# A two-layer gated mixer and expert kernel: half of the first parameters as a TensorE row, their slots loaded earlier, norms moved into the attention sweeps and from GpSimd to VectorE

## What is computed

```python
c_act = jax.nn.silu(c)
for l in range(DEPTH):
    mod = c_act @ ada_w[l] + ada_b[l]
    sh1, sc1, gt1, sh2, sc2, gt2 = jnp.split(mod, 6, axis=-1)
    h = modulate(rmsnorm(x, norm_mix[l]), sh1, sc1)
    proj = h @ w_in[l]
    y_a = hgrn2_mixer(...)   # gated linear recurrence
    y_b = mla_mixer(...)     # latent attention, rmsnorm of q and k per head, then rope
    y_c = diff_mixer(...)    # differential attention, rmsnorm of q, k and of the output
    y_d = swa_mixer(...)     # sliding window, rmsnorm of q and k
    merged = jnp.sum(sigmoid(gates) * branch, axis=2)
    x = x + gt1 * (merged @ w_out[l])
    h2 = modulate(rmsnorm(x, norm_ffn[l]), sh2, sc2)
    x = x + gt2 * moe(h2, ...)
```

## Time and profile before

| | us |
|---|---|
| median of 3 runs (2461.95 to 2464.5) | 2462.12 |
| the profiled execution | 2463.01 |
| its span (first to last instruction) | 2461.3 |
| PE busy | 2312.6 |
| DVE busy | 1416.3 |
| ACT busy | 1004.6 |
| POOL busy | 495.6 |

### The profile page before, as it was taken

The page is one execution under the profiler, slowest core; times in us unless marked ns, Lnnn a source line. Parts: engine busy times, 40 slices in busy tenths (PEclk is TensorE's granted clock), DMA queues, the critical chain, the costliest instruction groups (busy, mean ns, idle before and its releaser), DMA issues.

```text
span 2461.3 us, 33198 instructions
## 1 busy us (share of the span) xinstructions
PE 2312.6 (94%) x12222; PEld 1761.7 (72%) x12222; DVE 1416.3 (58%) x2621; ACT 1004.6 (41%) x1865; POOL 495.6 (20%) x457
## 2 busy tenths in 40 slices
PE   5999999988899999999989999999798999999997
PEld 4897787886575466777668978778766744677775
DVE  6637765554644634666486376654555455356664
ACT  2523333534443123666424233344444422246662
POOL 1002235011000210444200023330200022014440
PEclk9999999999999999999999999999898999999999
DMA  8322232231216653766272222321221284526652
GB/s 254 101 80 73 81 100 80 71 108 56 73 56 219 214 195 123 278 236 239 100 250 88 82 77 87 121 73 59 75 78 56 77 287 161 222 94 252 242 193 109
DMA packets 202110, 333.73 MB, mean 136 GB/s; under 512 B 31200, under 2 KB 162144, under 8 KB 185696
## 3 DMA queue, kind: packets, MB, share of 16 engines
q1 hardware_dynamic: 179024, 305.32, 36.5%
q0 software_dynamic: 19296, 19.98, 2.6%
q10 hardware_dynamic: 3632, 6.31, 0.7%
HBM read 352.48 MB, written 51.38 MB: 164 GB/s over the span
## 4 chain that ended last, share of the span: by engine, by line
PE 82%; DVE 7%; ACT 3%; issue 2%; SPq 2%; DMA 2%; POOL 1%; POOLq 0%; DVEq 0%; ACTq 0%
PE ps L733 77%; PE ps L731 6%; DVE ring_rounded L1799 1%; SPq L569 1%; DVE ssq L1911 1%; DMA ring<-in_ada_w 1%; DVE nmax L1936 1%; SPq L592 1%; DVE spare L1781 0%; DVE H L1894 0%; DVE H_rounded L1904 0%; DVE ps L1933 0%; DMA ring<-in_w_in 0%; ACT WH_rounded L1364 0%; DVE SQKV L1913 0%
## 5 line engine op out<-in xcount | busy, mean ns | idle before, releaser
L733 PE MATMUL ps<-H_rounded,WH_rounded 128*128 128x512 f32 x768 | 308.4, 402 | 0.0
L733 PE MATMUL ps<-X_rounded,WH_rounded 128*128 128x512 f32 x640 | 287.2, 449 | 9.9 <-DVE ring_rounded L1799 3.6
L1799 DVE TENSOR_TENSOR ring_rounded<-ring,WH_rounded 128x512 fp32r<-128x512 f32 (+2 forms) x168 | 198.2, 1188 | 152.9 <-ACT WH_rounded L1364 152.1
L733 PE MATMUL ps<-WH_rounded,X_rounded 128*128 128x256 f32 (+1 forms) x960 | 273.0, 284 | 6.9 <-issue 6.9
L733 PE MATMUL ps<-ring_rounded,X_rounded 128*128 128x256 f32 (+1 forms) x960 | 271.2, 282 | 0.0
L733 PE MATMUL ps<-WH_rounded,H_rounded 128*128 128x256 f32 (+1 forms) x960 | 271.1, 282 | 0.0
L733 PE MATMUL ps<-X_rounded,ring_rounded 128*128 128x512 f32 x640 | 253.5, 396 | 0.0
L1364 ACT ACTIVATE WH_rounded<-ring 128x512 fp32r<-128x512 f32 (+2 forms) x168 | 163.6, 983 | 184.9 <-PE ps L733 66.9
L733 PE MATMUL ps<-Y,ring 128*128 128x512 f32 x512 | 221.2, 593 | 1.9 <-ACT Y L1462 1.9
L733 PE MATMUL ps<-lmask,ident 128*128 128x256 f32 x784 | 190.8, 400 | 5.1 <-issue 3.1
L733 PEld LDWEIGHTS ps<-WH_rounded,X_rounded 128*128 128x128 f32 x960 | 184.1, 192 | 9.7 <-issue 9.6
(11 more groups left out here) (365 smaller groups left out, 4552.6 us busy)
## 6 DMA issues: line engine op xcount, KB each, us to landing
ring<-in_w_in SPq DMA_DIRECT2D x272, 256.0 KB, 3.9
ring<-in_ada_w SPq DMA_DIRECT2D x128, 256.0 KB, 4.9
Y<-in_moe_w_down SPq DMA_DIRECT2D x18, 1024.0 KB
ring<-in_w_branch SPq DMA_DIRECT2D x64, 256.0 KB, 5.2
ring<-in_moe_w_down SPq DMA_DIRECT2D x14, 1024.0 KB, 7.1
gate_logits<-CM SPq DMA_DIRECT2D x44, 256.0 KB, 2.6
...
```

Source lines behind the costliest of these rows:

```text
L733: ins = nc.tensor.matmul(o, lhsT, rhs, start=start, stop=stop)
L1799: ins = v.tensor_tensor(low[j][:, at:at + size], ring[:, j, at:at + size], high[i][:, at:at + size].bitcast(F32), ALU.subtract)
```

## The change

**Start of a layer.** The columns of shift stay with DVE (`ada` with two pairs instead of four); the columns of scale are made by PE as a row: `mod_part` multiplies one column of `cact` by 256 columns of a slot, eight matmuls a slot, four slots; ACT copies the row out of banks 7 and 6; `row_section` turns it into columns. The columns of the eight slots are dealt anew (`ADA_COLUMNS`). For layer 1, slots 0 to 3 are loaded by SP at the end of layer 0's expert stage, ahead of the rows that it loads back, and DVE's first pair and PE's first part are done there.

**Norms.** All gain multiplications and rope go to DVE (`weigh_by`, `rope`, with tables of `rope_tables`); for q and k pairs the two gains are multiplied once and applied to k alone. The norms `dif_norm`, `swa_norm` and `dif_post` leave `SCHEDULE` and are done inside the sweeps (`NORM_IN_SWEEP`), as is the pair `("ada", 3)` (`ADA_IN_SWEEP`, one k step every second unit).

**Banks and order.** `mla_turn` uses banks 2 to 5 in place of 2 and 3, without dummy matmuls between; product `c` 5 moves ahead of `turn` 2; `swa_turn` moves behind the sweep DIFF; `ada_keys(3, 2)` comes ahead of `d` in the ring.

```diff
 SCHEDULE = [("hg_norm", 0), ("c", 0), ("ada", 0), ("c", 1), ("hg_y", 0), ("c_norm", 0), ("ada", 1), ("c", 2),
             ("c_turn", 0), ("up", 0), ("c", 3), ("up", 1), ("turn", 0), ("c", 4),
-            ("up", 2), ("turn", 1), ("up", 3), ("turn", 2), ("section", 2), ("ada", 2), ("c", 5), ("turn", 3),
-            ("sweep", MLA), ("dif_norm", 0), ("d", 0), ("dif_norm", 1), ("ada", 3), ("d", 1), ("dif_norm", 2),
-            ("d", 2), ("dif_norm", 3), ("mla_y", 0), ("swa_norm", 0), ("swa_norm", 1),
-            ("swa_norm", 2), ("section", 3), ("swa_norm", 3), ("dif_turn", 0), ("swa_turn", 0),
-            ("sweep", DIFF), ("dif_post", 0), ("sweep", SWA), ("dif_y", 0), ("swa_y", 0)]
-WARM = {("c", 2): 4, ("up", 0): 7, ("turn", 2): 5, ("d", 2): 22}
+            ("up", 2), ("turn", 1), ("up", 3), ("c", 5), ("turn", 2), ("section", 2), ("ada", 2), ("turn", 3),
+            ("sweep", MLA), ("d", 0), ("d", 1), ("mla_y", 0), ("d", 2), ("section", 3), ("dif_turn", 0),
+            ("sweep", DIFF), ("swa_turn", 0), ("sweep", SWA), ("dif_y", 0), ("swa_y", 0)]
+WARM = {("c", 2): 5, ("up", 0): 7, ("turn", 2): 2, ("turn", 3): 3, ("c", 1): 3}
...
...
               + [("c", 4), ("c", 5)] + ada_keys(3, 0) + gate_keys("mla")
-              + [("d", 0), ("d", 1)] + ada_keys(3, 2) + [("d", 2)] + gate_keys("diff") + gate_keys("swa")
+              + ada_keys(3, 2) + [("d", 0), ("d", 1), ("d", 2)] + gate_keys("diff") + gate_keys("swa")
...
+ADA_COLUMNS = (0, 1, 4, 5, 2, 3, 6, 7, *range(8, 24))
+NORM_IN_SWEEP = {"mla": {23: ("dif_norm", 0), 25: ("dif_norm", 1), 27: ("dif_norm", 2), 29: ("dif_norm", 3)},
+                 "diff": {1: ("swa_norm", 0), 2: ("swa_norm", 1), 3: ("swa_norm", 2), 6: ("swa_norm", 3),
+                          9: ("dif_post", 0), 12: ("dif_post", 1), 15: ("dif_post", 2)},
+                 "swa": {3: ("dif_post", 3)}}
+ADA_IN_SWEEP = {8 + 2 * k: k for k in range(8)}
...
@@ sync: behind the expert weights, ahead of y_two @@
+                if l + 1 < DEPTH:
+                    for i in range(RING):
+                        ring_at = {j: at for at, j in slot_ring.items()}[ring_place(l + 1, ("ada", i))[0]]
+                        b, m = max(at for at in RELEASES if (3 * at[0] + at[1]) % SLOTS == ring_at)
+                        eng.wait_ge(expert_used, p.so_far(expert_used) - len(RELEASES) + RELEASES.index((b, m)) + 1)
+                        alone()
+                        ada_load(l + 1, ("ada", i))
...
@@ tensor @@
+            def mod_part(l, n):
+                half, i = divmod(n, 2)
+                b = 7 - half
+                w, used = slot(row_keys(half)[i], l)
+                w = heads(w, NC)
+                if i == 0:
+                    free(b)
+                for k in range(NC):
+                    ins = mm(ps[0:1, b, i * 256:(i + 1) * 256], cact[:, k:k + 1], w[:, k], k == 0, k == NC - 1,
+                             last=i == 1 and k == NC - 1)
...
+            def row_section(b):
+                free(b)
...
+                for m in range(NC):
+                    ins = mm(ps[:, b, m:m + 1], mod_row[:, tt(m)], ones[0:1, 0:1], last=last)
...
                 if l == 0:
                     warm(4, 5)
+                    for n in range(2):
+                        mod_part(0, n)
                 for c in range(NC):
                     square_sum(c)
-                for s in range(2):
-                    warm(((7, 37), (22, 30))[l][s], 5)
-                    section(1, s)
+                for n in range(2 if l == 0 else 1, 4):
+                    mod_part(l, n)
+                warm(3, 5)
+                section(1, 1)
+                row_section(1)
...
+                if l + 1 < DEPTH:
+                    mod_part(l + 1, 0)
                 for t in range(NT):
-                    warm((20, 2, 2, 2)[t], 7)
+                    warm((13 if l + 1 < DEPTH else 20, 2, 2, 2)[t], 2)
...
@@ tensor, mla_turn @@
                 for f in range(4):
-                    b = 2 + f % 2
-                    if f == 2 and t in (0, 1):
-                        warm((5, 8)[t], 5)
+                    b = 2 + f
...
@@ vector, in sweep @@
+                    if s.kind == "mla" and n in ADA_IN_SWEEP:
+                        ada(3, 2, ks=[ADA_IN_SWEEP[n]])
...
+                    if n - 1 in NORM_IN_SWEEP[s.kind]:
+                        norm_in_sweep(*NORM_IN_SWEEP[s.kind][n - 1])
...
+            def norm_in_sweep(step_, t):
+                head_norm(*norm_of(step_, t))
+                if step_ == "dif_norm":
+                    weigh_by(heads(DQK[:, t, 512:1024], 8), repeat(row("diff_qk_norm", 0, HD), 8), gained)
+                elif step_ == "swa_norm":
+                    weigh_by(heads(SQKV[:, t, 512:640], 2), repeat(row("swa_qk_norm", 0, HD), 2), gained)
+                else:
+                    weigh_by(heads(y_tok["diff"][:, t], DH), repeat(row("diff_onorm"), DH), gained)
...
@@ vector, do: hg_norm, c_norm, up @@
+                        head_norm(*norm_of(step_, t))
+                        weigh_by(heads(hgO[:, t], HEADS), repeat(row("hg_onorm"), HEADS), vector_step)
+                        eng.wait_ge(vector_step, p.given(vector_step))
+                        weigh_by(hgO[:, t], TM[:, t, 512:1024], gained)
...
+                    head_norm(*norm_of(step_, 1))
+                    weigh_by(CM[:, :, QR:QR + KVR], repeat(row("mla_kv_norm"), NT), gained)
+                    rope_tables()
...
+                    weigh_by(qk[:, HEADS:, 0:NOPE], repeat(row("mla_qk_norm", 0, NOPE), HEADS), vector_step)
+                    rope(qk, i)
```

200 lines of the change are left out of this document (105 added, 95 removed).

## The result

| | before | after |
|---|---|---|
| median, us | 2464.5 (2458.56 to 2469.11, 7 runs) | 2451.57 (2444.28 to 2452.13, 7 runs) |
| ratio, 95% interval | | 0.9942 (0.9929 to 0.9955) |
| PE busy in the span, us | 2312.6 of 2461.3 | 2293.7 of 2450.4 |
| POOL busy, us | 495.6 | 341.5 |
| share of PE in the chain that ended last | 82% | 79% |

Faster, as forecast, but by 0.6% where 1.7% was forecast: 2451.57 us lies above the range of 2397 to 2446. To find out where the rest went I read the starts and ends of the stages from the timelines of PE in both traces (first and last matmul of each), for both layers. The forecast stands beside each.

A forecast was written before the change was run, and what follows sets the result against it. PE was taken as the bound (82% of the last chain). Per layer -23.9 - 9.5 + 5.0 + 4.5 + 3.3 + 5.1 = -15.5, twice -31.0, with layer 1's start -40.5: 2421.5 us, range 2397 to 2446.

The forecast's parts named there:

- From MLA to DIFF, minus 23.9: MLA's last values to DIFF's first scores: without norms, PE's work runs together, 74.0 us become 50.1, per layer.
- Moving one pair of ada slots up in the ring is free by the same reason: Weight ring: d 1's slot, though freed only when the sweep ends, is ready within d 0's 11.8 us; cost nothing.
- SWA, minus 9.5: First four SWA units: 19.1 us become 9.1, with 0.5 kept for dif_post 3, per layer.
- Norms in MLA, plus 5.0: Late MLA units: four norms make PE wait about 1.3 us in each of three, 1.1 at the end; bounds 0, 14.8.
- Norms in DIFF, plus 4.5: DIFF sweep: four swa_norms at 0.6 us and three dif_posts at 0.7, per layer; between 0 and 18.
- rival "slower": Norms in sweeps cost full length because ACT holds the next exponentials back: 51 us more in all, 2472.5 us; chance 0.05.
- Ahead of MLA and the clock, plus 8.4: Per layer, the 124.9 us stretch before MLA grows by 3.3; lower clock after four waits there adds 5.1.
- rival "it hides better": Waits ahead of MLA and the clock's price are nil: 16.8 us less, 2404.8 us; chance 0.25.
- DVE without POOL: hg_norm, ahead of MLA: with POOL silent, the two slow roots on DVE fall from 1.75 to 0.7 us.
- Start of layer 1, minus 9.5: Start of layer 1: with four slots loaded before, the first projection comes at 1272.8 us instead of 1282.3.
- rival "the last rows are stored late": End of layer 0: POOL's store stands behind DVE's 6.2 us pair, layer 1 up to 5 us later, 2426.5; chance 0.05.
- Start of layer 0: 0 forecast: Start of layer 0: nothing loaded ahead, first projection 0.4 us earlier by the same steps, booked as 0.

The follow-up runs named there:

- roots_deferred: The changed kernel with each norm in a sweep cut in two, ACT's root behind the next unit's exponentials, DVE's sums and products later: 2419.38 us, ratio 0.9805.
- split_later: The changed kernel with the split of d 0 in the sweep MLA at units 22 to 25 instead of 18 to 21: 2446.15 us, ratio 0.9932.
- norms_undone: The changed kernel with the twelve norms back in SCHEDULE, 22 dummies ahead of d 2 and swa_turn ahead of DIFF again: 2483.61 us, ratio 1.0075.
- rows_first: The changed kernel with SP loading the experts' rows at the end of layer 0 ahead of ada slot 3 instead of behind it: 2447.06 us, ratio 0.9923.

## Why the prediction was wrong, point by point

**From MLA to DIFF, minus 23.9: mechanism right, 4 us too much.** The order is as read: d 0, d 1, mla_y, d 2 and the transposes in one piece. But I had taken each of the pieces at the full clock and mla_y without a wait. The two first products took 24.8 us for 23.5 at a clock of 0.83 in the first 11.7 us, ACT's copies made mla_y wait 1.66 us, and d 2 began at the half clock. Where PE arrives with its clock, the gap was 45.2 us (roots_deferred, layer 1); I had 45.4. The 4 us are those of this execution: other kernels with undeferred roots have 46.1 to 49.7.

**"Moving one pair of ada slots up in the ring is free by the same reason": this step failed.** I checked only that d 1 has its weights in time. d 0's own slot moved behind a gate slot that is freed inside the sweep, and what waited was not the product but ACT's split of it, with the exponentials behind. It cost 5.7 us in layer 0 and 0.9 in layer 1, where the transfer landed sooner; in four of the other kernels it cost about 1 in layer 0 too (split_later).

**SWA, minus 9.5: right**, 11.1 and 12.3; I had kept 0.5 for dif_post 3, and nothing of it shows. The 12.3 rest on the 98.9 us of one execution; norms_undone, where this sweep stands as before, has 97.7 and 97.6.

**Norms in MLA, plus 5.0: nearly right, its end too small.** 7.1 and 6.8. The walk through the first three norms costs what I had, 3.4 us for 3.9. Behind the last unit's scores it is 3.7 and 3.4, where I had 1.1: the last norm holds the last exponentials back, and the last values take 3.23 us for 2.07 at a falling clock. With the roots deferred all of it but 0.4 is gone.

**Norms in DIFF, plus 4.5: this step failed.** I scaled the price from MLA by width. 8.7 and 9.8 were measured, and most of it comes from two places, not from seven: the third swa_norm (a unit of 7.1 us for 5.0) and dif_post 1 (a unit of 8.8 for 6.0, and the next, at the low clock, of 9.2 for 7.4). What I had missed is the length of the way to DVE's sum: behind the next unit's row maxima, the weighing and a tile's copy. The mechanism was the one of my rival "slower" (ACT holds the next exponentials back); I gave it 0.05 because I weighed it as all or nothing. In fact it took a part, and roots_deferred shows its size, MLA and the clock that follows included: 32 us.

**Ahead of MLA and the clock, plus 8.4: right.** Measured 7.1 and 6.5 with the first units. c 1 waits 2.84 us (2.6 forecast), c 5 waits 3.96 (3.6), the first row maximum is 5 us late. The rival "it hides better" fell with it.

**DVE without POOL: right.** Timeline of DVE, hg_norm in the changed kernel: the second root's product, 1.75 us before, is

```profile
309.53 0.69 DVE L1979 TENSOR_TENSOR Y<-Y,rsq 128x512 f32<-128x512 f32 x1 [0.61 <-ACT rsq L1508]
...
312.88 0.69 DVE L1979 TENSOR_TENSOR Y<-Y,rsq 128x512 f32<-128x512 f32 x1 [0.61 <-ACT rsq L1508]
```

0.69, as the first. The Trainium skill (SBUF — State Buffer, section "two separate sides") says that DVE and GpSimd lock each other out of a shared port pair; the trace agrees: beside POOL's 1.28 us the instruction took 1.75, with POOL silent 0.69.

**Start of layer 1, minus 9.5: a third of it.** Minus 5.8 at the start, plus 2.8 ahead of it. Three sizes were off. The transfer of slot 3 delayed the rows by 2.6 us (1.5 booked; rows_first). The squares took 1.6 us longer and the last part 1.8, at half the clock. And from part 3 to the first projection 11.8 us passed, not 10.4 (the terms that I name there add up to 9.6). The clock's share belongs to the execution: in the six other kernels with the same code from the end of layer 0 to this projection the squares take 7.5 us, in five of them the last part 3.6, and the two stages together are 2.9 to 6.8 us shorter than before. The rival "the last rows are stored late" had the right place and the wrong cause: the store was done 1.2 us later, but behind slot 3's transfers and not behind DVE's pair, and the load took 1.7 us longer as well.

**Start of layer 0: 0 forecast, plus 1.5 in this execution.** The same code reached the first projection between 71.7 and 75.8 us in the profiles of the nine runs that leave it alone. All of them are later than the 70.9 of the kernel before, which has one profile only. So some 3 us were probably lost here that no term had; the cause stays open.

**The clock.** The 5.1 was about right ahead of MLA. That a clock lost in one stage is paid in the next, as in the gap, was in no term. All in all the misses in these two profiles are 8 us in the gap, 9.5 in DIFF, 6.6 for d 0's split, 4 for the norms in MLA and 6.5 at the start of layer 1, against 4 too little for SWA and 3 too much ahead of MLA.

What stays open: the gain from moving the gains off POOL was seen in the lengths of single instructions only; no kernel was run with them on POOL and all else as after. Nor was the row tried against DVE's way for layer 0 alone. And no kernel had the ada pairs in their old places with all else as after, though norms_undone shows that the change without its norms costs 18 us.
